# Two-layer backbone with experts: the norms' affine parts and the modulation as per-partition scale and offset on ScalarE, and the next layer's first chunks behind the experts

## Chip, cores, metric

One core of a Trainium2 chip. The metric is the device time of one execution in microseconds, the median of the runs. The core's engines work from queues of their own: TensorE (PE in the profile, its weight loads PEld), VectorE (DVE), ScalarE (ACT), GpSimd (POOL) and SyncE (SP), which here only issues DMA. They meet in semaphores. All data is float32.

## What is computed

256 latent tokens (`x`) and 256 context tokens (`ctx`), 1024 wide, go through two layers. `c` and `c_ctx` give the modulation vectors of the two streams. The reference, cut:

```python
for l in range(DEPTH):                     # DEPTH = 2
    mod_x = (c_act @ w_ada[l] + b_ada[l])[:, None, :]      # 6 vectors of 1024
    mod_c = cc_act @ w_ada[l] + b_ada[l]
    sh1, sc1, g1, sh2, sc2, g2 = jnp.split(mod_x, 6, axis=-1)
    px = _modulate(x, sh1, sc1) @ w_in[l]                  # h * (1 + scale) + shift
    ...   # Fourier mixer | differential attention | spatial gating -> mix_x
    x = _layernorm(DEEPNORM_ALPHA * x + g1 * (mix_x @ w_out[l]), ln_g[l, 0], ln_b[l, 0])
    ...   # the same for ctx, but in the last layer
    hx = _modulate(x, sh2, sc2)
    yx = _moe(hx, _route(hx, w_router, router_bias), moe_w1[l], moe_w3[l], moe_w2[l])
    x = _layernorm(DEEPNORM_ALPHA * x + g2 * yx, ln_g[l, 1], ln_b[l, 1])
return x
```

`_layernorm` subtracts the mean, divides by the root of the variance and applies `* g + b`, its affine part. `_moe` sends each token to 2 of 16 experts.

## The kernel before

**Tiling.** The tokens lie in `X` as four tiles of 128 rows (0 and 1 latent, 2 and 3 context); `tiles(L)` is 4 in layer 0 and 2 in layer 1, whose context output nobody needs, though its keys and values are needed. A tile is scaled and shifted into `H` (`HR`), turned on TensorE in eight 128x128 pieces into PSUM, copied into `XT` by ScalarE, and then multiplied with weights. PSUM's eight banks go round by a plan (`plan_layer`, `make_plan`): a job is named ("hT", L, t, half), ("ada", L, chunk) and so on; `full` waits for a job's result, `read` for its bank to be read out.

**Weights** come through a ring of six slots of 2 MB (`ring_plan`, `SLOTS`), loaded by SyncE in the ring's order; a load waits until the last job on its slot is done. A layer uses 12 chunks of `w_ada` (512 columns each: 0 and 1 are shift 1, 2 and 3 scale 1, 4 and 5 gate 1, 6 and 7 shift 2, 8 and 9 scale 2, 10 and 11 gate 2), the five chunks q, k, g, f, v of `w_in`, two of `w_out`, and then the 16 experts, whose three weights of 2 MB use three slots each, two experts at a time. The first four chunks of layer 1 stand, before, ahead of layer 0's experts in the ring and on TensorE.

**Modulation.** A chunk product (L1301, L1305) leaves a row of 512 values for the two streams; VectorE or ScalarE copies it to `R4`; `spread` (L1291) multiplies it by a selecting column, which repeats it over 128 partitions, one product of 128x512 for each stream; ScalarE copies that (L703) to `SH`, `SCL` or `GT`, which lie in `RA`, `RB` and `RC`. VectorE scales a tile (`modulate`, L929), GpSimd adds the shift (`shift`, L587).

**Norms.** For each tile VectorE sums up (`stats`, L938 to L934), GpSimd takes the root (L574), VectorE normalises (L946) and multiplies by `ln_g` (L949), GpSimd adds `ln_b` (L579); the vectors lie spread in `LNR` (`KT`). `norm_steps` writes the order out by hand, the same on VectorE and GpSimd: for the norm after the experts, tile n's mixing stands ahead of tile n-1's normalisation and tile n-2's modulation.

**Experts.** After `route` (L1468) and some 60 small operations on VectorE, GpSimd scatters each token's modulated row to two places of the DRAM table `xg_rows` (L605, one issue for each tile and choice), waits, reads blocks of 32 rows back (L615), ScalarE stages them, TensorE turns them (L1510), multiplies up (L1520) and down (L1536), and GpSimd stores the results in `y_rows` (L619). In the end it gathers each token's two rows into `G2` (L658), and VectorE mixes them (L1252 to L1256). Both tables are filled once at the start from `X` (L670, L672).

## Time and profile before

| | us |
|---|---|
| median of 3 runs | 1348.96 |
| lowest and highest | 1346.81, 1351.88 |
| the profiled execution, its own time | 1349.48 |
| its span, first to last instruction | 1347.9 |

| engine | busy us | share of the span |
|---|---|---|
| TensorE, products | 1009.5 | 75% |
| VectorE | 371.5 | 28% |
| GpSimd | 333.1 | 25% |
| ScalarE | 249.2 | 18% |

The DMA engines moved 332.08 MB, 246 GB/s in the mean. The profile is one execution; its time stands half a microsecond over the median. A share of busy time is a mean over stages that have different limits, so it has to be read by stage: from the timeline of an engine (each row is one or more equal instructions, with the idle time ahead of them and what ended it), and from windows, which give the busy time of each engine in a stretch.

### The profile page before, as it was taken

How to read it: one execution, taken by the hardware profiler on the slowest of the kernel's cores; microseconds unless marked ns; L12 is line 12 of the kernel's file. 1: busy time of each engine (PE TensorE's matmuls, PEld its weight loads, DVE VectorE, ACT ScalarE, POOL GpSimd, SP SyncE). 2: the span in 40 equal slices, each digit the busy share in tenths (PEclk: the TensorE clock that was granted, in tenths of full speed). 3: DMA queues.
4: the chain of work that ended last, by engine and by line, in shares of the span. 5: the costliest groups of instructions: out<-in, count | busy, mean ns of one | idle time of the engine just before them, and what ended most of it. 6: DMA issues, size and time to landing. Idle time of an engine off the chain costs nothing.

```text
span 1347.9 us, 23928 instructions
## 1 busy us (share of the span) xinstructions
PE 1009.5 (75%) x8962; PEld 550.3 (41%) x8963; DVE 371.5 (28%) x780; ACT 249.2 (18%) x519; POOL 333.1 (25%) x521
## 2 busy tenths in 40 slices
PE   3799998999839989977766408998893666865860
PEld 0444655445415545544434204455333333432430
DVE  0420228245302122211111186215243111101215
ACT  0211129301212112211110101115300111201110
POOL 1400000113333434332231345000022222321333
PEclk9899999999869999998798658999995888987995
DMA  9992310734764766689899770331684799999952
GB/s 301 392 414 71 125 63 1 269 137 146 284 257 146 261 257 224 211 304 331 327 388 408 284 244 29 124 125 63 246 317 186 283 399 401 357 395 406 394 191 94
DMA packets 91426, 332.08 MB, mean 246 GB/s; under 512 B 12988, under 2 KB 15164, under 8 KB 66804
## 3 DMA queue, kind: packets, MB, share of 16 engines
q1 hardware_dynamic: 68436, 282.05, 55.2%
q0 software_dynamic: 21472, 48.27, 10.5%
q10 hardware_dynamic: 1472, 1.12, 0.3%
q8 instruction: 32, 0.52, 0.2%
q14 instruction: 14, 0.11, 0.0%
HBM read 303.88 MB, written 27.53 MB: 246 GB/s over the span
## 4 chain that ended last, share of the span: by engine, by line
PE 60%; DMA 15%; issue 9%; DVE 8%; POOL 3%; SPq 3%; ACT 2%; POOLq 0%; DVEq 0%; ACTq 0%
PE PS L1520 18%; PE PS L1345 15%; DMA W<-in_moe_w 10%; PE PS L1536 7%; PE PS L1457 6%; PE PS L1510 3%; PE PS L1316 2%; PE PS L1301 2%; DMA xg_rows<-H,DEST 2%; PE PS L1528 1%; SPq L534 1%; PE PS L1291 1%; DMA X<-in_ctx 1%; ACT EX L785 1%; PE PS L1468 1%
## 5 line engine op out<-in xcount | busy, mean ns | idle before, releaser
L1520 PE MATMUL PS<-W,XT 128*32 128x256 f32 x4224 | 284.7, 429 | 114.9 <-DMA W<-in_moe_w 62.9
L1520 PEld LDWEIGHTS PS<-W,XT 128*32 128x32 f32 x4224 | 153.6, 123 | 224.5 <-issue 156.5
L619 POOL DMA_DIRECT2D y_rows<-H x264 | 130.9, 497 | 383.1 <-DVE H L1194 356.2
L1345 PE MATMUL PS<-W,XT 128*128 128x512 f32 (+1 forms) x544 | 218.3, 562 | 2.7 <-ACT RB L703 1.8
L1345 PEld LDWEIGHTS PS<-W,XT 128*128 128x128 f32 x544 | 104.1, 193 | 111.7 <-issue 109.4
L1536 PE MATMUL PS<-W,AT 128*32 128x256 f32 x2112 | 130.6, 389 | 3.6 <-DVE AT L1191 3.6
L1184 DVE COPY EX<-PS 128x256 f32<-128x256 f32 x66 | 28.0, 424 | 338.8 <-PE PS L1520 338.8
L703 ACT ACTIVATE H<-H 64x512 f32<-64x512 f32 x70 | 44.1, 631 | 361.3 <-PE PS L1510 318.5
L1510 PE MATMUL PS<-C,H 64*128 64x64 f32 x272 | 46.1, 291 | 66.7 <-ACT H L703 36.2
L615 POOL DMA_DIRECT2D H<-xg_rows x148 | 73.7, 501 | 74.0 <-issue 32.9
L1457 PE MATMUL PS<-W,XT 128*128 128x512 f32 x192 | 83.1, 593 | 0.0
L595 POOL TENSOR_TENSOR RSTD<-VAR,HALF 128x1 f32<-128x1 f32 (+1 forms) x12 | 9.6, 804 | 289.0 <-DVE VAR L934 289.0
L1536 PEld LDWEIGHTS PS<-W,AT 128*32 128x32 f32 x2112 | 63.3, 111 | 43.1 <-issue 5.7
L1510 PEld LDWEIGHTS PS<-C,H 64*128 64x128 f32 x272 | 37.6, 209 | 96.0 <-issue 96.0
L1301 PE MATMUL PS<-W,CT 128*32 128x512 f32 x384 | 53.1, 676 | 23.4 <-DMA W<-in_w_ada 23.4
L703 ACT ACTIVATE XT<-PS 128x512 f32<-128x512 f32 (+1 forms) x46 | 23.4, 541 | 203.7 <-PE PS L1316 189.8
L1194 DVE COPY H<-PS 128x256 f32<-128x256 f32 x66 | 28.0, 425 | 112.1 <-PE PS L1536 112.1
L1457 PEld LDWEIGHTS PS<-W,XT 128*128 128x128 f32 x192 | 36.3, 190 | 45.0 <-issue 45.0
L1187 DVE COPY XT<-PS 128x256 f32<-128x256 f32 x68 | 28.9, 424 | 88.3 <-PE PS L1510 88.3
L1316 PE MATMUL PS<-C,EX 128*128 128x128 f32 x88 | 16.0, 299 | 46.0 <-DMA EX<-in_sgu_w 33.7
L587 POOL TENSOR_TENSOR H<-H,RA 128x1024 f32<-128x1024 f32 x14 | 36.4, 2607 | 45.7 <-DVE H L929 45.7
L703 ACT ACT_TABLE_LOAD x18 | 23.1, 1283 | 122.1 <-PE PS L1510 122.1
(170 smaller groups left out, 920.7 us busy)
## 6 DMA issues: line engine op xcount, KB each, us to landing
W<-in_moe_w SPq DMA_DIRECT2D x96, 2048.0 KB, 14.3
W<-in_w_ada SPq DMA_DIRECT2D x24, 2048.0 KB, 13.5
W<-in_w_in SPq DMA_DIRECT2D x8, 2048.0 KB, 17.1
H<-xg_rows POOLq DMA_DIRECT2D x148, 64.0 KB, 5.7
y_rows<-H POOLq DMA_DIRECT2D x264, 32.0 KB, 5.2
W<-in_w_out SPq DMA_DIRECT2D x4, 2048.0 KB, 9.8
xg_rows<-X POOLq DMA_DIRECT2D x1, 6656.0 KB, 31.1
y_rows<-X POOLq DMA_DIRECT2D x1, 4608.0 KB, 46.8
```

Of the source, the lines that this page charges most:

```text
L587: pool.tensor_tensor(HR[:, t, :], HR[:, t, :], SH[:, t // 2, :], ALU.add).then_inc(S[h + "_ready"], 1)
L615: pool.dma_start(XRAW[b][ROWS * q:ROWS * q + ROWS, :], part_of_rows(xg_rows, n, slice(512 * q, 512 * q + 512))) .then_inc(rows_in[b][L], 16)
L619: pool.dma_start(part_of_rows(y_rows, n, slice(256 * q, 256 * q + 256)), YO[b][ROWS * q:ROWS * q + ROWS, :]) .then_inc(y_written[b][L], 16)
L703: nc.scalar.activation(dst, src, ACT.Copy).then_inc(done, 1)
L1187: dve.tensor_copy(XGT, ROWS_PS[:, 0:8 * ROWS].rearrange("p (k s) -> p k s", k=4)).then_inc(xgt_ready[L], 1)
L1301: mm = pe.matmul(ps[a:a + 32, :], CT[:, k, :], w[:, k, :], start=(k < 4), stop=False, tile_position=(0, a))
L1316: mm = pe.transpose(ps[:, P * n:P * n + P], piece, IDENT)
L1345: mm = pe.matmul(ps[:, 0:cw], XT[:, k, P * t:P * t + P], w[:, k, :], start=(k == 0), stop=(k == KD - 1))
L1457: mm = pe.matmul(ps, XT[:, k, P * t:P * t + P], w[:, k, :], start=(k == 0), stop=(k == KD - 1))
L1510: mm = pe.transpose(ROWS_PS[:, 2 * ROWS * k:2 * ROWS * k + 2 * ROWS], turned[:, k, :], IDENT[0:2 * ROWS, 0:2 * ROWS])
L1520: mm = pe.matmul(UP_PS[o:o + ROWS, 0:256], rows, moe_up(3 * p + n)[:, k, 256 * a:256 * a + 256], start=(k == 0), stop=(k == KD - 1), tile_ ...
L1536: mm = pe.matmul(DOWN_PS[o:o + ROWS, 0:256], rows, moe_down(3 * p + 2)[:, k, 256 * q:256 * q + 256], start=(k == 0), stop=(k == FE // P - ...
```

## The change

The scale and offset of a modulation become columns: one value for each of the 128 features that lie on the partitions once a tile is turned. So the raw tile of `X` is turned, and ScalarE applies both when it copies each 128x128 piece out of PSUM (`modulated`). For a tile that comes out of a norm, the norm's `ln_g` and `ln_b` are folded into them. The chunks 4, 5, 10 and 11, the gates, are still spread to rows; the other eight become columns by four products of two columns each (`spread`, `columns`).

`X` itself is only normalised (L976 of the changed kernel). Its affine part and the factor ALPHA are applied later, by two passes of VectorE on each tile (`residual`): after the router in both layers, and in layer 1 after the rotations. The rows for the scatter are got by turning `XT` back (jobs "hx") and copying them to `HR` on ScalarE. The last norm of all applies its affine part in two passes on VectorE. GpSimd has no passes over tiles left. ScalarE weighs the first of the two gathered rows (`weigh`). The first four chunks of layer 1 are loaded and multiplied behind the experts of layer 0. The group weights ("ab", "swT") stand ahead of the chunks in layer 0 and behind the first projections in layer 1. The norm vectors for the second norm are loaded within the experts (`load_ln`), and the fills of the tables no longer stand behind four shifts on GpSimd.

```diff
@@ ring_plan, plan_layer
     for L in range(DEPTH):
-        if L == 0:
-            for c in range(4):
-                put(("ada", L, c))
+        for c in range(4):
+            put(("ada", L, c))
...
         put(("ada", L, 10)), put(("ada", L, 11))
-        for c in range(4 if L + 1 < DEPTH else 0):
-            put(("ada", L + 1, c))
...
-    if L + 1 < DEPTH:
-        jobs += ada([0], L + 1)
+    jobs += [("hx", L, t, hf) for t in range(T) for hf in range(2)]
     jobs += [("rk", L), ("ct", L)]
-    if L + 1 < DEPTH:
-        jobs += ada([1, 2, 3], L + 1)
@@ SyncE
+            for n, vec in enumerate((ln_g, ln_b)):
+                o = 2 * DEPTH * KD * n
+                sp.dma_start(LNV[o:o + 2 * DEPTH * KD, :], vec.rearrange("l j (k p) -> (l j k) p", p=P)).then_inc(ln_cols_in, 16)
...
-                    sp.wait_ge(done, steps_of_layer(sp, L0))
+                    sp.wait_ge(done, steps_of_layer(sp, L0) if s >= 3 else steps_before(sp, L0, NEXP - 1))
@@ GpSimd
+            def load_ln(L, j):
+                if j:
+                    pool.wait_ge(S["affine"], val("affine", L, 0))
+                pool.dma_start(LNR[:, 0, :], ln_g[L, j].partition_broadcast(P)).then_inc(ln_in, 16)
+                pool.dma_start(LNR[:, 1, :], ln_b[L, j].partition_broadcast(P)).then_inc(ln_in, 16)
...
-                if L == 0:
-                    for t in range(4):
-                        shift("h1", 0, t)
...
+                load_ln(L, 1)
                 pool.wait_ge(meta_ready, L + 1)
...
                 for t in range(T):
                     if t >= 2:
+                        rstd(req(L, "ln2", t - 2), 1)
                         pool.wait_ge(S["mixed_ready"], val("mixed_ready", L, t - 2))
@@ ScalarE
+            def modulated(key, kind, t):
+
+                ps = full(act, key)
+                hf = key[3]
+                for k in range(4):
+                    n = 4 * hf + k
+                    ins = nc.scalar.activation(XT[:, n, P * t:P * t + P], ps[:, P * k:P * k + P], ACT.Identity,
+                                               bias=MB[:, kind, n, t // 2:t // 2 + 1], scale=MA[:, kind, n, t // 2:t // 2 + 1])
+                ins.then_inc(freed(key), 1)
...
+                g0 = G2[:, t % 2, 0, :]
+                nc.scalar.activation(g0, g0, ACT.Copy, scale=WK2[:, t, 0:1]).then_inc(weighed, 1)
...
+                if L:
+                    ada_rows(L, [0, 1, 2, 3])
+                    weigh(L - 1, 0)
+                    weigh(L - 1, 1)
...
+                gates(L, [10, 11])
+                for t in range(T):
+                    for hf in range(2):
+                        key = ("hx", L, t, hf)
+                        copy(HR[:, t, 512 * hf:512 * hf + 512], full(act, key), freed(key))
@@ VectorE
-                link(dve.tensor_scalar(X[:, t, :], X[:, t, :], MV[:, t, 0:1], RSTD[:, r, 0:1], ALU.subtract, ALU.mult))
...
+                dve.tensor_scalar(X[:, t, :], X[:, t, :], MV[:, t, 0:1], RSTD[:, r, 0:1], ALU.subtract, ALU.mult)\
+                    .then_inc(done, 1)
+
+            def residual(L, j, t):
+
                 dve.wait_ge(ln_in, 32 * (2 * L + j + 1))
-                dve.tensor_tensor(X[:, t, :], X[:, t, :], LNR[:, 0, :], ALU.mult).then_inc(done, 1)
+                link(dve.scalar_tensor_tensor(out=X[:, t, :], in0=X[:, t, :], scalar=ALPHA, in1=LNR[:, 0, :],
+                                              op0=ALU.mult, op1=ALU.mult))
+                return dve.scalar_tensor_tensor(out=X[:, t, :], in0=LNR[:, 1, :], scalar=ALPHA, in1=X[:, t, :],
+                                                op0=ALU.mult, op1=ALU.add)
...
+                for t in range(T):
+                    mix(t)
+                    if t == 0 and L + 1 < DEPTH:
+                        for c_ in range(4):
+                            columns(L + 1, c_)
+                    normalise(L, "ln2", t, S["ln2_norm"])
@@ TensorE
+                if not is_row(c_):
+                    ps, done = claim(("col", L, c_))
+                    for m in range(4):
+                        mm = pe.matmul(ps[:, 2 * m:2 * m + 2], R4[:, c_ % 2, P * m:P * m + P], cst("sel"), start=True, stop=True)
+                    mm.then_inc(done, 1)
+                    return
...
-                            turn(("hT", L, t, hf), [HR[:, t, 512 * hf + P * k:512 * hf + P * k + P] for k in range(4)])
+                            turn(("hT", L, t, hf), [X[:, t, 512 * hf + P * k:512 * hf + P * k + P] for k in range(4)])
```

**Three places in the order.** First SyncE's loads from layer 0's chunks 4 to 9 to the experts, before and after; W is the ring, in_w_ada the chunks, in_moe_w the experts' weights.

```order
L534 DMA W<-in_w_ada 128x8x512 x6
L534 DMA W<-in_w_out 128x8x512 x2
L534 DMA W<-in_w_ada 128x8x512 x6
L491 DMA W<-in_moe_w 128x2x2048 x6
L510 UNCONDITIONAL_BRANCH
```

```order
L538 DMA W<-in_w_ada 128x8x512 x6
L538 DMA W<-in_w_out 128x8x512 x2
L538 DMA W<-in_w_ada 128x8x512 x2
L492 DMA W<-in_moe_w 128x2x2048 x6
L514 UNCONDITIONAL_BRANCH
```

Four loads, layer 1's first chunks, are gone from ahead of the experts' first six; they stand now behind the loop's end.

Second, TensorE from the last tile's turning (PS<-C,H, then PS<-C,X) to the experts' first turned rows (PS<-C,H 128x64); GATE marks the rank and count products.

```order
L1316 MATMUL PS<-C,H 128x128 x8
L1468 MATMUL PS<-WR,XT 128x16 x16
L1301 MATMUL PS<-W,CT 32x512 x8
L1305 MATMUL PS<-BA,C 32x128 x4
L1291 MATMUL PS<-R,C 128x512 x2
L1493 MATMUL PS<-GATE,C 128x16
...
L1497 MATMUL PS<-GATE,C 128x16 x4
L1301 MATMUL PS<-W,CT 32x512 x8
L1305 MATMUL PS<-BA,C 32x128 x4
```

```order
L1363 MATMUL PS<-C,X 128x128 x8
L1526 MATMUL PS<-WR,XT 128x16 x16
L1363 MATMUL PS<-C,XT 128x128 x32
L1552 MATMUL PS<-GATE,C 128x16
...
L1556 MATMUL PS<-GATE,C 128x16 x4
L1567 MATMUL PS<-C,H 128x64 x4
```

The chunk products on either side of the ranks are gone, and 32 turnings of XT, the rows for the scatter, stand in the place of the first.

Third, VectorE at the handover, from the first gathered tile; G2 lies in H, WK holds the two weights of a token, MA, MB and SHC are the columns.

```order
L1252 TENSOR_SCALAR H<-H,WK 128x1024
L1253 SCALAR_TENSOR_TENSOR H<-H,WK 128x1024
L1255 TENSOR_TENSOR H<-H,RC 128x1024
L1256 SCALAR_TENSOR_TENSOR X<-X,H 128x1024
L938 BN_STATS ST<-X 128x6 x2
L940 BN_AGGR MV<-ST 128x2
L934 TENSOR_SCALAR VAR<-MV 128x1
...
L946 TENSOR_SCALAR X<-X,MV,RSTD 128x1024
L949 TENSOR_TENSOR X<-X,KT 128x1024
L1252 TENSOR_SCALAR H<-H,WK 128x1024
```

```order
L1297 SCALAR_TENSOR_TENSOR H<-H,WK 128x1024
L1299 TENSOR_TENSOR H<-H,RC 128x1024
L1300 TENSOR_TENSOR X<-X,H 128x1024
L961 BN_STATS ST<-X 128x6 x2
L963 BN_AGGR MV<-ST 128x2
L957 TENSOR_SCALAR VAR<-MV 128x1
L938 COPY SHC<-PS 128x8 x2
...
L953 TENSOR_TENSOR MB<-MB,SHC 128x8
L976 TENSOR_SCALAR X<-X,MV,RSTD 128x1024
L1297 SCALAR_TENSOR_TENSOR H<-H,WK 128x1024
```

Before, tile 1's seven rows stand where the dots are, ahead of tile 0's normalisation. After, only the eight small operations on the columns stand there, and tile 1 comes behind.

## Rows read from the trace of the kernel before

**Rows 1.** The page's part 4: the chain that ended last, shares by engine.
```profile
PE 60%; DMA 15%; issue 9%; DVE 8%; POOL 3%; SPq 3%; ACT 2%; POOLq 0%; DVEq 0%; ACTq 0%
```

**Rows 2.** Timeline of the start: start us, us, engine, line, operation, [idle before <-releaser].
```profile
42.69 8.92 DVE L929 SCALAR_TENSOR_TENSOR H<-RB,X 128x1024 f32<-128x1024 f32 x4 [3.64 <-DMA X<-in_ctx]
...
52.35 8.13 PE L1345 MATMUL PS<-W,XT 128*128 128x512 f32 x16
...
56.06 1.20 POOL L670 DMA_DIRECT2D xg_rows<-X  x1
```

**Rows 3.** The scatters: POOL's timeline, and in layer 0 the hardware queue of 355:400.
```profile
361.59 1.05 POOL L605 DMA_INDIRECT xg_rows<-H,DEST  x1 [20.43 <-issue]
...
389.57 0.60 POOL L615 DMA_DIRECT2D H<-xg_rows  x1 [18.11 <-DMA xg_rows<-H,DEST]
...
q1 hardware_dynamic: 851, 6.45, 35.9%
...
1043.65 2.07 POOL L615 DMA_DIRECT2D H<-xg_rows  x4 [3.35 <-DMA xg_rows<-H,DEST]
```

**Rows 4.** Timelines of the handover between the layers: PE and DVE.
```profile
735.30 3.66 PE L1520 MATMUL PS<-W,XT 128*32 128x256 f32 x64
...
777.92 0.75 DVE L1252 TENSOR_SCALAR H<-H,WK 128x1024 f32<-128x1024 f32 x1 [13.10 <-DMA H<-y_rows,DEST]
...
784.11 0.15 DVE L934 TENSOR_SCALAR VAR<-MV 128x1 f32<-128x1 f32 x1
...
792.70 0.81 DVE L946 TENSOR_SCALAR X<-X,MV,RSTD 128x1024 f32<-128x1024 f32 x1 [2.19 <-POOL RSTD L574]
...
795.48 3.25 DVE L1253 SCALAR_TENSOR_TENSOR H<-H,WK 128x1024 f32<-128x1024 f32 x1
...
811.11 1.97 PE L1316 MATMUL PS<-C,H 128*128 128x128 f32 x8 [13.73 <-POOL H L587]
813.96 9.67 PE L1345 MATMUL PS<-W,XT 128*128 128x512 f32 x16 [0.89 <-ACT XT L703]
...
843.75 41.48 PE L1345 MATMUL PS<-W,XT 128*128 128x512 f32 x112 [1.81 <-ACT RB L703]
```

**Rows 5.** Windows: stretch, length, busy of five engines, PEclk, DMA share, GB/s.
```profile
1080.00:1120.00 40.00, 20.17 (x282) 11.04 (x278) 4.70 (x12) 5.29 (x8) 10.20 (x21) 0.87 1.02 403
```

**Rows 6.** Loads of W issued by SyncE from 28 to 30: issue to landing.
```profile
DMA to landing us min/median/max: 19.7/21.7/23.6
```

**Rows 7.** Queues, packets, MB, share: from 60 to 61, then from 62 to 63.
```profile
q0 software_dynamic: 11, 0.05, 11.7%
...
q0 software_dynamic: 70, 0.29, 69.6%
q1 hardware_dynamic: 67, 0.14, 35.2%
```

**Rows 8.** PE's timeline in layer 0: chunk products, router, last tile, counts.
```profile
249.41 1.98 PE L1291 MATMUL PS<-R,C 128*128 128x512 f32 x4
...
312.37 1.86 PE L1468 MATMUL PS<-WR,XT 128*128 128x16 f32 x16
...
340.17 1.09 PE L1316 MATMUL PS<-C,H 128*128 128x128 f32 x8 [1.50 <-POOL H L587]
...
355.34 1.87 PE L1497 MATMUL PS<-GATE,C 128*128 128x16 f32 x8
```

**Rows 9.** ACT's timeline: one 128x128 piece out of PSUM with a scale.
```profile
943.25 0.37 ACT L803 ACTIVATE RB<-PS,RI 128x128 f32<-128x128 f32 x1
```

**Rows 10.** PE's timeline at the router of layer 1.
```profile
1013.63 1.94 PE L1316 MATMUL PS<-C,H 128*128 128x128 f32 x8 [4.91 <-POOL H L587]
1015.36 6.85 PE L1468 MATMUL PS<-WR,XT 128*128 128x16 f32 x32
```

**Rows 11.** The end: DVE's first pass and POOL's last.
```profile
1323.79 0.75 DVE L1252 TENSOR_SCALAR H<-H,WK 128x1024 f32<-128x1024 f32 x1 [13.13 <-DMA H<-y_rows,DEST]
...
1342.45 2.34 POOL L579 TENSOR_TENSOR X<-X,KT 128x1024 f32<-128x1024 f32 x1 [1.16 <-DVE X L949]
```

More of the change, by code:

```diff
@@ L65 @@
 COUNTS = {
-    "h1_ready": lambda L: 4,
     "q_rot": lambda L: 2, "k_rot": lambda L: 2,
@@ L415, in backbone, with g_wait @@
         passed = sem("passed")
+        def g_wait(eng, L, t):
+            eng.wait_ge(g_in[t % 2], 32 * (sum(tiles(l) for l in range(L)) // 2 + t // 2 + 1))
         def wait_apart(eng, semaphore, value):
@@ L979, in _ @@
                 dve.tensor_copy(SWT[:, :, :].rearrange("p a b -> p (a b)"), full(dve, key)).then_inc(freed(key), 1)
+            key = ("lnc", 0)
+            dve.tensor_copy(LNC[:, :, :, :, :].rearrange("p a l j k -> p (a l j k)"), full(dve, key)[:, 0:4 * DEPTH * KD])\
+                .then_inc(freed(key), 1)
+            group_weights(0)
+            ada_copy(0, 0)
+            for c_ in range(1, 4):
+                ada_copy(0, c_)
+                columns(0, c_ - 1)
+            columns(0, 3)
+            for L in range(DEPTH):
+                T = tiles(L)
                 if L == 0:
@@ L994, in _ @@
                     rotate(KR, t).then_inc(S["k_rot"], 1)
+                if L:
+                    for t in range(T):
+                        read(dve, ("hT", L, t, 1))
+                        residual(L - 1, 1, t)
+                    group_weights(L)
                 for t in range(4):
@@ L1181, in _ @@
                 dve.tensor_copy(META[0:1, L, 2, 0:2], T2[0:1, :]).then_inc(halves_ready, 1)
+                for t in range(T):
+                    for hf in range(2):
+                        read(dve, ("xT", L, t, hf))
+                    ins = residual(L, 0, t)
+                ins.then_inc(S["affine"], 1)
                 def copy_up():
@@ new lines, in _, with mix @@
+                for c_ in (10, 11):
+                    for r in mod_streams(L, c_):
+                        read(dve, ("mod", L, c_, r))
+                def mix(t):
+                    g_wait(dve, L, t)
+                    dve.wait_ge(weighed, sum(tiles(l) for l in range(L)) + t + 1)
+                    g0, g1 = G2[:, t % 2, 0, :], G2[:, t % 2, 1, :]
+                    link(dve.scalar_tensor_tensor(out=g0, in0=g1, scalar=WK2[:, t, 1:2], in1=g0,
+                                                  op0=ALU.mult, op1=ALU.add))
+                    link(dve.tensor_tensor(g0, g0, GT[:, t // 2, :], ALU.mult))
+                    dve.tensor_tensor(X[:, t, :], X[:, t, :], g0, ALU.add).then_inc(S["mixed_ready"], 1)
+                    dve.wait_ge(S["mixed_ready"], val("mixed_ready", L, t))
+                    stats(L, "ln2", t)
```

311 lines of the change are left out of this document (143 added, 168 removed).

## The prediction

> **What bounds the kernel now.** I read the chain of waits first [rows 1]: TensorE carries 60% of it, DMA 15%, time in which nothing is seen to hold an engine 9%, VectorE 8%. So the kernel is mostly bound by the products, and I looked for the stretches where TensorE stands still, in the timeline of each engine. Five lie near the edit. (a) The start: the first projection begins at 52.35, although the tokens are in SBUF at 42.69 [rows 2]. (b) The two router stages, where the last tile's rows come late. (c) The scatter of the rows to the experts: in layer 0 first issue 361.59, rows read back 389.57; in layer 1 read back at 1043.65 [rows 3]. (d) The handover between the layers: TensorE turns the first rows of layer 1 only at 811.11, after 13.73 us of its last wait for GpSimd [rows 4]. (e) The end. Within the experts of layer 1 the bound is another: the DMA engines are 1.02 busy with 403 GB/s from 1080 to 1120 [rows 5]. That stream is driven by the products (a slot is reloaded when its expert is done), so experts that start earlier also end earlier.
>
> **Start.** Four scalings on VectorE (8.92 us together) and four additions on GpSimd lay between the tokens and the first turned rows [rows 2]. Now X itself is turned, and the scale and shift ride on ScalarE's copies out of PSUM. With the tokens at 42.7 two tiles are turned and tile 0 copied by about 47. The next wait is the weights of the chunk q. Their load was issued at 28.39 and took the shortest landing of its pair, 19.7 us, so 48.1 [rows 6]. And two things push it later. The two small loads of the norm vectors stand ahead of the weights on SyncE's queue: 0 to 1 us, I take 0.8. The two fills of the row tables, issued at 56.06 before [rows 2], now follow the tokens directly, at about 43. Between 60 and 61 their queue moved its first 0.05 MB, so bytes come about 4.5 us after the issue; between 62 and 63 it moved 0.29 MB and the weights' queue 0.14, packet for packet, so the weights keep a third [rows 7]. From 47.5 on the fills thus meet the last 1 us of q's load, which then takes 3. That puts q at 50.6 and the gain at **1.7**. Ends: q at 46.5 would be 5.8, and fills that move at once would give q at 56, a loss of 4.
>
> **Chunk products of layer 0 (4 to 9).** Six chunks each carried a spreading to rows of 1.98 us in two streams. Chunks 4 and 5, the gate, keep it. Chunks 6 to 9 become four products with 2 columns each. The nearest row is the router's, 128x128 by 16 columns: 1.86 us for 8 products, each in two passes [rows 8], so 0.93 for 4, and 0.85 net of overlap. Four times 1.98-0.93, all on TensorE's path: **4.2**. In layer 1 there is one stream, half of the row, so about **0.6**.
>
> **Router of layer 0.** TensorE waited 1.50 for GpSimd before the last tile [rows 8]; that goes, but ScalarE's part grows: a 128x128 piece with a scale takes 0.37 [rows 9], eight are 2.96 in the place of two copies. I take +0.7 (0 to 1.5). Then the rank and count products run after a pause, in which the chunk products had kept the clock up. In the trace the counts, 8 passes, took 1.87 while the router's 16 took 1.86 [rows 8], so a pass doubles; the 20 rank passes would lose 1.6. Together **-0.9**. The eight turned-back halves (hx) and their copies run beside VectorE's routing chain and cost nothing while they are done before the destinations, which come after the counts of 355.34 [rows 8].
>
> **Scatter of layer 0.** From the first issue to the rows read back there are 28.0 us, 9.9 of issues and 18.11 of waiting; in layer 1 the wait was 3.35 [rows 3]. The difference is 6.45 MB of weights that ran on the hardware queue in that stretch [rows 3]: three of the first six expert slots were held by the chunks of layer 1, which stood there. Now these chunks come behind the experts, so the six slots are filled as chunks 8 to 11 and the two output chunks are used, all before the last tile is turned at 340.17 [rows 8]; even four loads of 2 MB from there, at 400 GB/s [rows 5], are over by 361. The scatter then has the engines alone: 9.9 of issues, 3.35, and 1.0 for bytes that fall behind the issues over twice the tiles, 14.3. The gain is **13.7** (7 to 15). What is late next is VectorE: it now multiplies X by the norm's vectors and ALPHA there, 2 passes a tile. Eight passes at about 1.3 (tile 0's 6.3 us of mixing and statistics in [rows 4] hold five such steps) are 10 us, done before the rows are read back. If each took 3.25, as one does beside GpSimd's own work [rows 4], they would last 26 and end 12 us late.
>
> **Handover.** Before, tile 0's rows were there at 777.92 and its statistics done at 784.26 [rows 4], 6.3 us later; then the normalisation waited until 792.70, since it stood behind tile 1 on VectorE and behind two gathers on GpSimd, and scaling, offset, modulation and shift of four tiles shared the two engines, one of VectorE's passes growing to 3.25 [rows 4]. After: gathered rows at 779.3 (1.4 later, since 14 MB of weights are now asked for instead of 6 and share the engines); the first weighting on ScalarE 1.1 (bounds 0.75, VectorE's time for it [rows 4], and 2.96); the rest of the mix and the statistics 5.5; eight small column operations 2; normalisation 0.81. Turned rows at 788.9 instead of 811.1. From turned rows to the first projection it took 2.85 and now 4.4 (the eight pieces), so 793.3 instead of 813.96: 20.7. From there to the 112 records at 843.75 it took 29.8, of which 27 were products (9.67, two of 7 and three turnings of 1.1); tiles now follow each other every 7.2 us on VectorE against 8 on TensorE, so about 2.9 of waits go, and the group products that had stood in the idle time, 1.7, come in. Sum **21.9** (12 to 27). Cover: the four chunk products must be done by then. Their loads no longer wait for the last expert: the first two leave when expert 14's up product is done, 739.0 [rows 4], the next after its down product, which I put 16 us later; two loads of 5.1 us at 400 GB/s [rows 5] bring the fourth chunk by about 769, some 10 before the gathered rows, and q by 781. SyncE's loads of the chunks f and v wait for the gathers as before.
>
> **Router of layer 1.** TensorE turned the last rows at 1013.63 after waiting 4.91 for GpSimd, and the router products took 6.85 for 32 records, twice the rate of [rows 8], at the lower clock after the pause [rows 10]. Now the rows are there before the chunk products end, so 4.9 go; without a pause the products take 3.7, another 3.1; ScalarE's pieces and the first half's overlap give net 0.1. **8.1** (4 to 9).
>
> **Norm vectors.** Their second load, 1 MB, ran in the idle DMA of the router stage; now it is issued behind the third store of the experts. In layer 0 there is room; in layer 1 the stream is full [rows 5], and 1 MB at 400 GB/s is **-2.6** (0 to -3.5).
>
> **End.** From gathered rows at 1323.79 to the end of GpSimd's last addition, 1342.45+2.34, there are 21.0 [rows 11]. After: 1.1 of ScalarE, then per tile 5.5, about 1.2 for the root, and two passes of 1.25, 18.4 for both tiles, 19.5 in all, **+1.3**.
>
> **The sum.** 1.7+4.2+0.6-0.9+13.7+21.9+8.1-2.6+1.3 = 48.0. The profiled execution took 1349.5, half a microsecond above the median of the runs, so I forecast 1301.5 and round to **1301**.
>
> **Rule against trace.** The scatter issues of [rows 3] ran with VectorE idle, about 1.05 each, and no row shows one beside a pass over X, as they now stand. The Trainium skill (SBUF — State Buffer, A bandwidth-pool intuition that's wrong, and the box on the DVE blocking DMA) says that a DMA issued from GpSimd needs descriptors which GpSimd can't write while VectorE holds the shared port in a 2-port mode. By that rule in its widest reading each issue waits for one pass, 1301 would become 1311 to 1316, and the first rival below goes by it; its page names copies and tensor-scalar forms, not these.
>
> **Rivals.** (1) VectorE's passes collide with GpSimd's scatter issues, either way round. Eight issues held back by 1.25 each are 10 us in layer 0 and 5 in layer 1, or the passes grow to 3.25 and end late by as much. For it: the 3.25 of [rows 4]. Against it: that one came beside GpSimd's arithmetic. Time 1311 to 1316. (2) Layer 1 waits for its chunk weights: gathers, stores and 14 MB share the engines, and TensorE's and ScalarE's queues stand behind the fourth chunk. If the weights keep a third of 400 [rows 7] from 755 on, 4 MB take 31 us, the fourth chunk lands near 786, and 10 to 13 us of the handover are lost: 1311 to 1314. (3) The handover is better than this: the rows come no later, and the start gains 5: 1288 to 1294. (4) **Slower than before**: the wait of (2) taken to its end. ScalarE must copy four chunks before it may weigh tile 0, and VectorE needs their columns before it normalises; every microsecond by which the fourth chunk lands after 776 (its product and copy take some 3) is one on the path. It decides from 48 us past that, a landing at 824; one at 860 gives 1385. Only a slot that is released late could do it; the 14 MB queued there are 35 us of bytes from 739, which speaks against it. (5) The change doesn't do what it says: the slots are released no earlier than before, or VectorE's passes eat the gain: 1343 to 1354.
>
> **How the numbers follow.** Forecast, 1293 to 1309: 0.61. Rival 1: 0.09; rival 2: 0.13; rival 3: 0.10; both 1 and 2 or half the handover, 1316 to 1342: 0.02; rival 4: 0.02; rival 5: 0.03, of which 0.02 within the bound. The range, 1290 to 1317, takes in the forecast, rivals 1 and 2 and part of 3, with the ends of the scatter, the start and the handover. What a measurement of this kernel can tell from no change is 0.5%, 6.7 us. Faster 0.95, same 0.02, slower 0.03.
>
> **What would show it.** In the changed kernel's timeline: the first projection near 50 and its release by DMA; rows read back 14 us after the first scatter issue in layer 0, with no weights on the hardware queue; layer 1's first turned rows at 11 to 12 us after the gathered rows; no pass of 3.25 on VectorE; router records of layer 1 at half the time; the distance of the last gather to the end 1 to 2 us shorter. Wrong would be: a 128x128 piece on ScalarE far above 0.37, TensorE waiting for in_w_ada in the handover, or VectorE not done when the first rows of the experts are turned.

## The result, and the profile after

The changed kernel takes **1298.61 us** (median of four runs, 1297.23 to 1299.59) against 1349.88 in the same rounds (1346.81 to 1351.88): a ratio of 0.9635, 95% interval 0.961 to 0.9661. A second timing (x_ref below) gave 1295.57 and 0.9604 (0.9586 to 0.9621). The forecast was 1301, range 1290 to 1317, and faster. The profiled execution took 1297.62 with a span of 1296.0, so 51.9 of span are gone where the sum had 48.0.

Put beside each other, the marks of the two traces give this (us; each is the distance between two marks before, less the same distance after):

| step | forecast | the two traces |
|---|---|---|
| start, up to the chunk products of layer 0 | 1.7 | 2.8 |
| chunk products, layer 0 | 4.2 | 4.2 |
| router, layer 0 | -0.9 | -0.5 |
| scatter, layer 0, to the first turned rows | 13.7 | 12.3 |
| experts, layer 0 | (0) | 7.9 |
| handover, from the first gather to the end of layer 1's attention | 21.9 | 22.3 |
| chunk products, layer 1 | 0.6 | 1.2 |
| output projection and router, layer 1 | 8.1 | 5.5 |
| scatter, layer 1 | (0) | -1.7 |
| experts, layer 1 | -2.6 | -4.4 |
| end | 1.3 | 2.3 |

The page's chain of the changed kernel, which answers to [rows 1]: VectorE has lost half of its share, GpSimd a third, and DMA has grown.

```profile
PE 63%; DMA 17%; issue 9%; DVE 4%; SPq 3%; ACT 2%; POOL 2%; POOLq 0%; DVEq 0%; ACTq 0%
```

The marks are, in order: TensorE's first chunk product of layer 0 behind the attention, its first output projection product, GpSimd's first scatter issue, the experts' first turned rows, the first gather's issue, and the same again in layer 1, up to the span's end.

The start, in the timelines of GpSimd (the first fill) and TensorE (the first projection); [rows 2] had them at 56.06 and 52.35.

```profile
42.76 1.18 POOL L664 DMA_DIRECT2D xg_rows<-X  x1 [35.18 <-DMA X<-in_ctx]
...
47.62 10.01 PE L1398 MATMUL PS<-W,XT 128*128 128x512 f32 x16 [2.67 <-DMA W<-in_w_in]
```

The projection is 4.7 sooner and released by its weights, as forecast, but at 47.6 and not at 50.6. It then ran slower (10.01 for 16 products against 8.13), which took a part back.

The scatter of layer 0, GpSimd's timeline and under it three of VectorE's eight residual passes; it answers to [rows 3].

```profile
355.11 1.75 POOL L597 DMA_INDIRECT xg_rows<-H,DEST  x1 [30.12 <-issue]
357.16 2.00 POOL L597 DMA_INDIRECT xg_rows<-H,DEST  x1 [0.30 <-issue]
359.46 0.95 POOL L597 DMA_INDIRECT xg_rows<-H,DEST  x1 [0.30 <-issue]
360.71 0.95 POOL L597 DMA_INDIRECT xg_rows<-H,DEST  x1 [0.30 <-issue]
361.97 1.97 POOL L597 DMA_INDIRECT xg_rows<-H,DEST  x1 [0.30 <-issue]
...
371.12 2.08 POOL L607 DMA_DIRECT2D H<-xg_rows  x4 [3.42 <-DMA xg_rows<-H,DEST]
```

```profile
354.68 1.23 DVE L982 SCALAR_TENSOR_TENSOR X<-X,KT 128x1024 f32<-128x1024 f32 x1
...
357.08 1.22 DVE L982 SCALAR_TENSOR_TENSOR X<-X,KT 128x1024 f32<-128x1024 f32 x1
...
361.90 1.21 DVE L982 SCALAR_TENSOR_TENSOR X<-X,KT 128x1024 f32<-128x1024 f32 x1
```

From 355 to 390 this queue moved all but 0.05 MB; the hardware queue, which had 6.45 MB in [rows 3], moved nothing:

```profile
q0 software_dynamic: 1808, 5.38, 44.7%
```

The wait for the scatter's bytes is 3.42 instead of 18.11, close to the 3.35 of layer 1 before. But three of the eight issues are 0.8 to 1.1 us longer than the 0.95 of their neighbours. VectorE's passes keep their 1.23 and are over at 364.4, 10.9 before VectorE is wanted.

The handover, in time: the third and the fourth chunk product (TensorE), its copy and the first weighting (ScalarE), the first turned rows and the first projection (TensorE). It answers to [rows 4].

```profile
743.04 3.54 PE L1348 MATMUL PS<-W,CT 128*32 128x512 f32 x16 [2.00 <-DMA W<-in_w_ada]
...
748.42 1.92 PE L1348 MATMUL PS<-W,CT 128*32 128x512 f32 x16 [0.50 <-DMA W<-in_w_ada]
```

```profile
750.76 0.60 ACT L688 ACTIVATE R<-PS 128x512 f32<-128x512 f32 x1 [3.16 <-PE PS L1352]
754.45 1.15 ACT L731 ACTIVATE H<-H,WK 128x1024 f32<-128x1024 f32 x1 [3.10 <-DMA H<-y_rows,DEST]
```

```profile
763.36 1.97 PE L1363 MATMUL PS<-C,X 128*128 128x128 f32 x8 [10.79 <-DVE X L976]
767.73 10.05 PE L1398 MATMUL PS<-W,XT 128*128 128x512 f32 x16 [2.40 <-ACT XT L718]
```

The first gather is issued at 744.50, so it is 18.9 us to turned rows, where it was 40.0 (771.16 to 811.11). The rows themselves come later after the issue, 9.95 instead of 6.76.

The experts, windows from the first turned rows to the first gather, both layers; columns as in [rows 5]. First the kernel before, then the changed one.

```profile
393.30:771.16 377.86, 299.01 (x4194) 173.70 (x4194) 66.03 (x172) 67.56 (x107) 127.68 (x258) 0.90 0.76 281
1047.27:1317.03 269.76, 183.18 (x2554) 102.58 (x2554) 39.55 (x101) 41.28 (x65) 76.34 (x155) 0.89 0.91 352
```

```profile
374.52:744.50 369.98, 297.09 (x4250) 166.32 (x4254) 65.97 (x172) 68.64 (x109) 128.86 (x260) 0.92 0.79 293
993.34:1267.48 274.14, 187.35 (x2554) 103.46 (x2554) 39.52 (x101) 42.56 (x66) 77.48 (x156) 0.87 0.90 351
```

The largest surprise is the first column after the stretch: 7.9 less in layer 0 and 4.4 more in layer 1, though the edit puts nothing into these loops but one load of norm vectors. The granted clock goes the same way, 0.90 to 0.92 and 0.89 to 0.87. Whether that is the kernel or the execution is what the first experiment asks.

### The profile page after: what moved, and what is told of

Its sections match the earlier page's. It is cut to its first block, busy times and chain, and to the rows that moved or that the text cites. A ratio compares the mean times of both kernels' runs of the same rounds, so it can differ in the third digit from the quotient of the medians.

```text
span 1296.0 us, 24219 instructions
## 1 busy us (share of the span) xinstructions
PE 1008.2 (78%) x9083; PEld 558.1 (43%) x9084; DVE 336.0 (26%) x795; ACT 271.3 (21%) x594; POOL 268.1 (21%) x495
## 4 chain that ended last, share of the span: by engine, by line
PE 63%; DMA 17%; issue 9%; DVE 4%; SPq 3%; ACT 2%; POOL 2%; POOLq 0%; DVEq 0%; ACTq 0%
PE PS L1577 17%; PE PS L1398 17%; DMA W<-in_moe_w 13%; PE PS L1593 7%; PE PS L1515 7%; PE PS L1567 3%; PE PS L1348 2%; PE PS L1363 2%; DMA W<-in_w_in 1%; PE PS L1585 1%; SPq L538 1%; POOL xg_rows L597 1%; DMA H<-y_rows,DEST 1%; ACT EX L785 1%; PE PS L1526 1%
## 5 line engine op out<-in xcount | busy, mean ns | idle before, releaser
L1577 PE MATMUL PS<-W,XT 128*32 128x256 f32 x4224 | 280.3, 424 | 116.3 <-DMA W<-in_moe_w 64.6
L1577 PEld LDWEIGHTS PS<-W,XT 128*32 128x32 f32 x4224 | 145.5, 122 | 229.8 <-issue 162.1
L580 POOL TENSOR_TENSOR RSTD<-VAR,HALF 128x1 f32<-128x1 f32 (+1 forms) x24 | 16.3, 683 | 480.1 <-DVE VAR L957 480.1
L718 ACT ACTIVATE XT<-PS,MB,MA 128x128 f32<-128x128 f32 x112 | 40.5, 470 | 142.4 <-PE PS L1363 142.4
L851 ACT ACTIVATE EX<-PS 128x128 f32<-128x128 f32 x66 | 18.3, 277 | 76.1 <-PE PS L1585 75.9
L1585 PE MATMUL PS<-C,EX 128*128 128x128 f32 x132 | 33.6, 337 | 0.0
```

Of the source, the lines that this page charges most:

```text
L718: ins = nc.scalar.activation(XT[:, n, P * t:P * t + P], ps[:, P * k:P * k + P], ACT.Identity, bias=MB[:, kind, n, t // 2:t // 2 + 1], scal ...
L1577: mm = pe.matmul(UP_PS[o:o + ROWS, 0:256], rows, moe_up(3 * p + n)[:, k, 256 * a:256 * a + 256], start=(k == 0), stop=(k == KD - 1), tile_ ...
L1585: mm = pe.transpose(TURN_PS[:, P * k:P * k + P], turned[:, k, :], IDENT)
```

## Experiments

All are edits of the changed kernel but for the second execution of the kernel before. Spans of a stretch are distances between the marks of the table.

**The same kernel twice more.** No edit.

> The changed kernel once more, without an edit, for a second profiled execution. Between the kernels before and after the products of the experts took TensorE 297.2 us before and 289.3 after in layer 0, and 183.2 before and 187.4 after in layer 1, with the same number of products. Theory A: which products fall into the lower clock follows from the kernel's own order and waits, so this execution shows 289.3 and 187.4 again, within 0.5. Rival B: it changes from execution to execution by single products of 1.7 to 2.5 us, and the two numbers differ from those by one or several of such steps.

> The kernel before once more, without an edit, for a second profiled execution. In four profiled executions in which the experts of layer 0 are word for word the changed kernel's, the time from their first turned rows to the first gather was 370.0, 372.2, 373.5 and 377.5 us; the one trace of before shows 377.9. Theory: this spread, of single products at the lower clock, covers the kernel before too, and this execution shows 370 to 378. Rival: before is slower there for a reason of its own, and it shows 377 to 379. In layer 1 (269.8 before, 272.5 to 274.1 after) the same question: 269 to 271 if the second norm vectors' load is what makes the difference, up to 274 if it is chance.

> The changed kernel without an edit, timed in the same rounds as the three kernels beside it, so that they can be compared with it and not only with the kernel before. Expected: 1296 to 1300, and in the profiled execution again three scatter issues of 1.7 to 2.0 us in layer 0 and two in layer 1, 16.0 and 9.9 from the first issue to the rows read back, 272 to 275 for the experts of layer 1, and for the experts of layer 0 anything from 370 to 378, since that varied so over eight profiled executions of the same instructions.

The same two windows of x_same:

```profile
373.39:745.56 372.17, 302.83 (x4262) 168.51 (x4266) 66.03 (x172) 68.75 (x109) 128.71 (x259) 0.91 0.79 293
992.79:1265.33 272.54, 187.59 (x2554) 103.53 (x2554) 39.57 (x101) 42.55 (x66) 77.47 (x156) 0.87 0.91 353
```

Theory A of x_same fell: layer 0 took 372.17 with TensorE busy 5.7 longer than in the first execution. Over the eleven profiled executions with the changed kernel's expert loops in layer 0, the stretch took 370.0 to 377.7, mean 374.5. The kernel before took 377.9 and, in x_before, 377.8. Chance is a large part of that spread: x_qgate and x_noln below run the changed kernel's instructions word for word up to the end of this stretch, and took 372.8 and 377.5. So the 7.9 of the table can't be read as a gain of the edit; the first trace is the shortest of the eleven. Nor is it shown to be chance alone. The three executions of the unedited changed kernel are the three shortest of the eleven (370.0, 370.7, 372.2), the two of before agree within 0.1, and the distance of the two means, 374.5 and 377.8, is some 3. How much of the 7.9 belongs to the kernel stays open.

The same holds for the output projection of layer 1. Its first 27 to 29 us, in the first trace and in x_same:

```profile
923.74:953.00 29.26, 29.26 (x67) 12.79 (x67) 7.11 (x14) 0.00 (x0) 0.56 (x1) 0.94 0.77 302
```

```profile
925.52:953.10 27.58, 27.58 (x67) 12.22 (x67) 7.11 (x14) 0.00 (x0) 0.56 (x1) 1.00 0.82 318
```

The same 64 products, TensorE without a pause in both, and a granted clock of 0.94 against 1.00: a part of that stretch ran at the lower of the two levels in one execution and not in the other. From the projection's start to VectorE's first routing operation it took 43.2 twice and 40.7 to 40.8 in nine executions, against 48.64 and 48.67 before. The term is then 7.9, where the forecast had 8.1 and the first trace seemed to say 5.5.

In layer 1's experts the difference is not chance, as the next experiment shows. x_ref again gave what was expected of it: 16.0 and 9.9 in the scatters, 370.7 and 272.9 in the experts.

**The norm vectors' second load left out in layer 1.**

```diff
-                load_ln(L, 1)
+                if L == 0:
+                    load_ln(L, 1)
...
-                    dve.wait_ge(ln_in, 32 * (2 * L + 2))
+                    dve.wait_ge(ln_in, 32 * (2 * L + 1))
```

> The changed kernel without the load of the second pair of norm vectors (1 MB) in layer 1; the last norm of the output is then done with the first pair's values, so that part is computed with other numbers. The prediction had priced this load at 2.6 us, as bytes in a full stream. Theory from the two traces: TensorE's idle time within the experts of layer 1 was 79.6 us before and 79.8 after, so the load costs nothing, and 1298 to 1299 comes out, with that idle time unchanged within 1 us. Rival, as predicted: 1 MB at 400 GB/s is on the path, the idle time falls by 2.6, and the time is 1296.

```profile
995.39:1265.94 270.55, 184.66 (x2554) 102.86 (x2554) 39.56 (x101) 42.55 (x66) 76.32 (x155) 0.88 0.90 351
```

1292.36 us, ratio 0.9582 (0.9567 to 0.9597). The experts of layer 1 took 270.55. With the load in the stream eight executions of them took 272.5 to 274.9 (mean 273.5); without it (this one, the two of before, x_clean and x_best, whose load stands ahead of the scatter) 269.8 to 271.8 (mean 270.9). The two sets don't overlap. The load costs about 2.6 us. The theory I had formed from the two traces, that it costs nothing since TensorE's idle time had not moved, was wrong; the term of the prediction, 2.6, was right. By the windows' first two columns, TensorE's idle time there was 87.2 in the mean of the eight and 85.6 in the mean of the five, its busy time 186.3 and 185.3: 1.6 of the price is idle time and 1.0 busy time. But single executions of the eight lay anywhere from 85.0 to 88.6 of idle time, so two traces could not show it. In time, 1292.36 is 3 to 6 us below the two timings of the changed kernel.

**The chunks ahead of the experts again.** The ring, the plan and the four products go back to their old places, the columns stay.

```diff
-        for c in range(4):
+        for c in range(4 if L == 0 else 0):
             put(("ada", L, c))
...
         put(("ada", L, 10)), put(("ada", L, 11))
+        for c in range(4 if L + 1 < DEPTH else 0):
+            put(("ada", L + 1, c))
```

> The changed kernel with its second part undone: the four chunk products of layer 1, their loads and their column operations stand ahead of the experts of layer 0 again, one before the ranks and three after the counts; the columns and the affine parts stay as they are. Theory: the shorter scatter of layer 0 comes from this move alone, since three expert slots are no longer held by the chunks. So from the first issue to the rows read back it takes 26 to 30 us instead of 16.0, and the experts' first rows are turned 10 to 14 later. At the handover the gathered rows come 1 to 3 sooner, since fewer weights are asked for with them. Together 1305 to 1312. Rival: the scatter became shorter because the norm vectors' loads left that stretch; then it stays at 16 and the time is 1296 to 1300.

GpSimd's timeline, and the hardware queue from 355 to 390:

```profile
363.97 1.95 POOL L603 DMA_INDIRECT xg_rows<-H,DEST  x1 [0.30 <-issue]
...
384.14 2.09 POOL L613 DMA_DIRECT2D H<-xg_rows  x4 [16.96 <-DMA xg_rows<-H,DEST]
```

```profile
q1 hardware_dynamic: 816, 6.29, 45.0%
```

1307.57 us, ratio 0.9692 (0.9677 to 0.9707). From the first issue to the rows read back it takes 27.9 instead of 16.0, with 6.29 MB of weights on the hardware queue, as in [rows 3]. From the routing's start to the first turned rows it is 50.5 against 36.6. Of these 13.9, 11.9 are the scatter and the other 2.0 lie before it, where a chunk product again stands ahead of the ranks. The gathered rows of the handover come 6.6 after their issue again. So the move brings the whole gain of the scatter and costs 3.3 at the handover. Only one issue is long here, since VectorE's first pass began only at 363.86.

**VectorE's passes away from the scatter,** in two steps. x_early takes all tiles' passes out of the scatter but the last one's:

```diff
                     normalise(L, "ln1", t, S["ln1_norm"])
+                    if t:
+                        for hf in range(2):
+                            read(dve, ("xT", L, t - 1, hf))
+                        residual(L, 0, t - 1)
...
-                for t in range(T):
-                    for hf in range(2):
-                        read(dve, ("xT", L, t, hf))
-                    ins = residual(L, 0, t)
-                ins.then_inc(S["affine"], 1)
+                for hf in range(2):
+                    read(dve, ("xT", L, T - 1, hf))
+                residual(L, 0, T - 1).then_inc(S["affine"], 1)
```

> The changed kernel with VectorE's two passes over X (norm vectors and ALPHA) taken out of the scatter: for all tiles but the last they stand behind the next tile's normalisation, beside the output projection, and only the last tile's two passes stay where they were. Theory: some of GpSimd's scatter issues took 1.75 to 2.0 us instead of 0.95 because VectorE ran these passes beside them. Three of eight in layer 0 and two of four in layer 1 would go back to 0.95, apart from one or two beside the last tile's passes: 1 to 2 us less in layer 0 and 0 to 1.7 in layer 1, so 1295 to 1297. Rival: the issues are long for another reason (the first ones after a long idle, or ScalarE's copies into the rows); they stay at 1.75 to 2.0 and the time is 1298 to 1299.

x_clean moves the last tile's too, ahead of the routing chain, and `load_ln(L, 1)` from the third store to a place before the scatter:

```diff
-                load_ln(L, 1)
...
                 rstds(L, "ln1")
+                load_ln(L, 1)
...
+                    for n in (t - 1, t) if t == T - 1 else (t - 1,) * (t > 0):
+                        for hf in range(2):
+                            read(dve, ("xT", L, n, hf))
+                        ins = residual(L, 0, n)
+                ins.then_inc(S["affine"], 1)
...
-                for t in range(T):
-                    for hf in range(2):
-                        read(dve, ("xT", L, t, hf))
-                    ins = residual(L, 0, t)
-                ins.then_inc(S["affine"], 1)
```

> The changed kernel with all of VectorE's residual passes ahead of the routing chain, the last tile's too (VectorE stands idle for 9 us there while the last tile is turned and its router product runs), and the load of the second norm vectors issued before the scatter, as in the kernel before, since those passes are over by then. Theory: no issue of the scatter is beside a pass any more (28.0 became 16.0 and now 14.3 in layer 0; 9.9 becomes 8.2 in layer 1), and the experts of layer 1, 272.5 to 274.1 with the load in them, take 270 to 271. Together 5 to 7 less than the changed kernel: 1291 to 1294. Rival: the passes ahead of the routing delay it by up to 2.5 in each layer, and the load of 1 MB, now ahead of the scatter, costs nothing there; then 1296 to 1298.

GpSimd's timeline in x_clean, the first issue and the read:

```profile
352.98 1.05 POOL L597 DMA_INDIRECT xg_rows<-H,DEST  x1 [14.51 <-issue]
...
366.96 2.10 POOL L607 DMA_DIRECT2D H<-xg_rows  x4 [4.09 <-DMA xg_rows<-H,DEST]
```

In x_early only the first issue of each layer stayed long (1.74 and 1.98), beside the last tile's passes; the scatters took 14.65 and 9.17. In x_clean none was longer than 1.05, and they took 13.98 and 8.24 instead of 16.0 and 9.92. The passes lay in VectorE's idle time: from the output projection's start in layer 0 to the first scatter issue it took 91.4 in x_clean and 92.8 in x_best, which has the same passes, and 91.6 to 93.6 in the executions with the passes left or moved less (x_ahead aside). In layer 1 the same stretch took 53.7 in both, against 53.6. The experts of layer 1 took 271.8. x_early was timed at 1297.24 (0.9614, 0.9593 to 0.9634), which the runs can't tell from the changed kernel; x_clean at 1293.47 (0.9587, 0.9563 to 0.9611), inside its theory, but its interval overlaps those of the changed kernel (0.961 to 0.9661 and 0.9586 to 0.9621). That it gains rests on the stretches of the trace.

**The fills later.**

```diff
                     pool.wait_ge(x_in, 32)
+                    pool.wait_ge(w_full[PLACE["in", 0, "q"][0]], 16 * PLACE["in", 0, "q"][1])
```

> The changed kernel with the two fills of the row tables issued only when the weights of the first projection have landed. Theory, as predicted: at the end of that load the fills share its queue's engines and stretch its last microsecond to three; without them the first projection starts 1.5 to 2.5 earlier, near 45, released by ScalarE's pieces at the soonest, and the time is 1.5 to 2.5 below the changed kernel's, 1294 to 1297. Rival: the load is late for its own queue (the ten loads ahead of it), and the start stays at 46.7 to 48.9, as in five profiled executions of the changed start.

TensorE's and GpSimd's timelines:

```profile
47.12 10.15 PE L1399 MATMUL PS<-W,XT 128*128 128x512 f32 x16 [2.21 <-DMA W<-in_w_in]
...
47.71 1.18 POOL L665 DMA_DIRECT2D xg_rows<-X  x1 [40.13 <-DMA W<-in_w_in]
```

1300.61 us, ratio 0.9634 (0.9609 to 0.966): nothing gained. The fills now start after the projection's weights are there, and the weights are there at the same time, 47.1, within the 46.7 to 48.9 of the other executions. So the fills are not what makes the load late. The rival's own cause, what stands ahead of the load on its queue, is what is left, but no run varied it.

**A later release of slots.**

```diff
-                    sp.wait_ge(done, steps_of_layer(sp, L0) if s >= 3 else steps_before(sp, L0, NEXP - 1))
+                    sp.wait_ge(done, steps_of_layer(sp, L0))
```

> The changed kernel with every expert slot released to layer 1's weights only after the last expert's step, as in the kernel before; the three slots of expert 14 thus wait one expert longer. Theory: the first chunk's load then leaves some 17 to 20 us later, the four chunks of 2 MB follow each other every 5.1, and the fourth, which landed at 748.4 with the rows weighed at 754.5, lands near 760. ScalarE copies the chunks ahead of its weighting, so the first weighting moves 7 to 11 back and the time is 1305 to 1310. Rival: the chunks' loads are not what the handover waits for (three of them go out at once when the step is over), and it is 1299 to 1302.

TensorE (the fourth chunk product) and ScalarE (the weightings):

```profile
765.12 3.64 PE L1348 MATMUL PS<-W,CT 128*32 128x512 f32 x16 [7.11 <-DMA W<-in_w_ada]
```

```profile
769.90 2.18 ACT L731 ACTIVATE H<-H,WK 128x1024 f32<-128x1024 f32 x2
```

1307.66 us, ratio 0.9685 (0.9663 to 0.9707). From the gather's issue to the weighting it took 17.7 instead of 9.2 to 10.5, and the weighting starts with the end of the fourth chunk's copy, not with a wait for the gathered rows. That copy ended 6.9 behind the gather's issue in the first trace and 17.8 here, 10.9 later; 3.1 were margin and the other 7.8 are on the path. This is the mechanism of the rival "slower than before" at a small dose, in this one dose one for one beyond the margin. The release of three slots one expert earlier, a single expression in the diff, is worth 8 us of the handover in the trace (167.9 up to layer 1's chunk products, against 159.6 to 160.1 in the three executions of the changed kernel) and 12 in the times of the same rounds (1295.57).

**The weights of q held back,** and both good edits together (x_best: x_clean and this one).

```diff
+                if key == ("in", key[1], "q") and key[1]:
+                    sp.wait_ge(g_in[0], 32 * (sum(tiles(l) for l in range(key[1] - 1)) // 2 + 1))
                 if key == ("in", key[1], "f") and key[1]:
```

> The changed kernel with one more wait on SyncE's queue: in layer 1 the weights of the chunk q, and so all behind them, are issued only when tile 0's two gathered rows have landed. Theory: from the first gather's issue to the weighting it took 9.6 to 10.0 us, against 6.8 in the kernel before and 6.6 with the chunks ahead of the experts, because the weights asked for early share the engines; with q held back it takes 7.5 to 8.5. q is then asked for near 753 and lands by 762, before the first projection of 767.7 can start, so 1.5 to 2.5 are gained: 1295 to 1297. Rival: q becomes late itself, the first projection waits for its weights instead of ScalarE, and the time is 1299 to 1305.

> The two edits that did what was expected, together: all residual passes ahead of the routing with the second norm vectors' load before the scatter, and the weights of q in layer 1 held until tile 0's rows have been gathered. Theory: they act in different places and add, 4 to 6 for the first and 1.5 to 3 for the second, so 1289 to 1293, with 14.0 and 8.2 in the scatters, 7.2 from the gather to the weighting and 270 to 272 in the experts of layer 1. Rival: the fourth chunk's copy, which stood directly ahead of the weighting in the execution with q held back, takes the gain of the second edit, and the time is that of the first alone, 1292 to 1295.

ScalarE's timeline, x_qgate and then x_best:

```profile
755.92 0.60 ACT L690 ACTIVATE R<-PS 128x512 f32<-128x512 f32 x1 [2.62 <-PE PS L1354]
756.41 1.14 ACT L733 ACTIVATE H<-H,WK 128x1024 f32<-128x1024 f32 x1
```

```profile
753.79 1.15 ACT L733 ACTIVATE H<-H,WK 128x1024 f32<-128x1024 f32 x1 [1.79 <-DMA H<-y_rows,DEST]
```

x_qgate: 1295.95 us (0.9606, 0.9582 to 0.963), with 7.2 from the gather's issue to the weighting. There the fourth chunk's copy was already what the weighting waited for. Its time can't be told from the changed kernel's; the gain is one of the trace. x_best: **1289.26 us** (six runs, 1285.56 to 1297.01; ratio 0.9557, 0.9529 to 0.9586), beside 1295.57 for the changed kernel in the same rounds; 14.0 and 8.2 in the scatters, 6.5 at the gather, 271.5 in the experts of layer 1. Against x_ref's trace its own stretches are 2.0+1.7+4.1+1.4 = 9.2 shorter, while the experts of layer 0 took 377.2 in that execution and 370.7 in x_ref's, the variation of above. It is clearly faster than the kernel before. Against the changed one it is 6.3 us in the medians, but the ends of the two intervals meet and single runs overlap.

## Why the prediction was right, and where it was not

**Start.** The direction and the releaser were right, the size not: 47.6 was measured where I had 50.6. The step that failed is "the weights keep a third": without the fills the load lands no sooner (x_fills), so they cost it nothing that shows. It was a loss computed from a rate 13 to 15 us later in the trace, [rows 7]; and by its own terms (48.1 and 0.8, bytes of the fills from 47.5) there were 1.4 us of load left to stretch and not 1, which gives 51.7. Over the executions the mark behind the start lies at 240.6 on the mean against 243.6 before, so 3.0.

**Chunk products and router of layer 0.** The 4.2 came out by luck in part: the four chunks' columns gave 3.6, and 0.6 came from the first chunk product of the stretch, which took 2.55 before and 1.92 after. The columns of a chunk took 1.05 for 8 passes where I had taken 0.93. The same holds for the 1.2 of layer 1, of which 1.0 is its first product (2.92 and 1.92), and it comes and goes between executions: the whole stretch took 19.3 in x_before and 20.4 in x_same. The router's -0.5 for -0.9 holds two errors that balance. 1.6 was gained up to the last turned tile (I had 1.5), then 1.4 was lost up to the ranks, where I had 0.7 for ScalarE's part, and the ranks lost 0.65, where I had 1.6. My own three terms add to -0.8.

**Scatter of layer 0.** The mechanism was right and is shown by x_ahead. The size was 12.3 instead of 13.7, 12.0 of it up to the rows read back: the wait after the issues was 3.4 and not 4.35, but the issues took 12.6 and not 9.9. That is the first rival, which I gave a chance of 0.09 at 10 to 15 us. It did happen, at 2.0 in layer 0 and 1.7 in layer 1 (x_clean), beside the forecast and not instead of it. I had treated it as a case that is there or not; it should have been a term with a size. Layer 1's part was nowhere in the sum. The rival's size failed as well: it had every issue wait for a whole pass, and three of eight waited for what was left of one.

**Handover.** 22.3 for 21.9. The pieces: weighting 1.15 (1.1), mixing and statistics 5.6 (5.5), columns 1.2 (2), turned rows to projection 4.4 (4.4). The rows came 3.2 later after their issue, where I had 1.4, and the columns gave 0.8 of that back, so 19.6 were gained up to the first projection for 20.7. The rest of layer 1's attention gave 2.7, where I had 1.2 (2.9 of waits less 1.7). The cover was thinner than I wrote: I had the fourth chunk some 10 before the gathered rows, and it was there 6 before, 3 with its product and copy. x_late shows what lay behind that margin. "TensorE waiting for in_w_ada in the handover" stood among the signs of being wrong, and it did wait, 2.00 and 0.50 us; it cost nothing, since the rows came 3.1 after the last copy. And the 11 to 12 us from gathered to turned rows, among the signs, doesn't follow from the sum, which has 9.6; 8.9 was measured.

**Router of layer 1.** 5.5 in the first trace, 7.9 in nine of eleven executions, for 8.1. **Norm vectors.** 2.6 forecast, about 2.6 measured over the executions; the 4.4 of the first pair holds 1.8 of chance. **Experts of layer 0.** No term of mine; 7.9 in the pair, and how much of it belongs to the kernel is open. **End.** 2.3 for 1.3: from the gathered rows to the last operation it took 18.9 where I had 19.5, since the second tile's weighting lay beside VectorE's work, and the last gathers came no later. The term was mis-subtracted too; 21.0 less 19.5 is 1.5.

So the sum, 48.0, came near to the 51.9 of the traces with errors that balanced by chance: the scatters gave 3.1 less than worked out, the first trace had the slow phase in the output projection against it (2.4), and it had 7.9 in its favour in a stretch in which one load was the only change. Over the three executions of the changed kernel the span is 51.9 to 54.2 below that of the first trace of before.

## What to carry to other kernels

When work for the next stage holds buffers that the present stage needs, moving it behind that stage can pay: here the slots were filled before the scatter, so that the scatter ran with no weights beside it (11.9 us). Look at once for what then shares the engines at the new place (3.3 us here), and for what must be released so that it arrives in time (12 us in x_late). Work that an engine takes over should lie where that engine is idle and where its neighbour issues no DMAs. And before a difference of a few us between two traces is explained, the same kernel is profiled again: here one stretch of some 374 us took from 370.0 to 377.5 in five executions that ran the same instructions up to its end.

## What the runs showed of the hardware

GpSimd's issue of an indirect DMA took 0.95 to 1.08 us beside no long VectorE pass. Beside the passes of `residual`, which read two streams of SBUF, it took 1.74 to 2.01 when it began 0.07 to 0.44 after the start of a pass (in the trace above 355.11 after 354.68, 357.16 after 357.08, 361.97 after 361.90; 363.97 after 363.86 in x_ahead; in layer 1 979.82 and 982.10, 0.20 and 0.07 after a pass). The excess is what was left of that pass: 0.8 left gave 1.75, 1.03 left gave 1.98, 1.15 left gave 2.01. Each of the 40 long issues in the nine traces that have them ended 0.82 to 0.96 after the end of the pass, the length of an undisturbed issue or a little less. So these issues looked blocked until the pass was over, and not slowed. An issue that began 0.01 ahead of a pass (359.46), or with less than 0.15 of one left, kept its 0.95 to 0.99, and the passes kept their 1.23.

The Trainium skill (SBUF — State Buffer, A bandwidth-pool intuition that's wrong, and the box on the DVE blocking DMA) says that GpSimd can't write descriptors while VectorE holds the shared port in a 2-port mode, which is the rule that the prediction named. The same page of the Trainium skill (Who interferes with whom) also has VectorE instructions with two SBUF inputs, which these passes are: they contend with a GpSimd instruction that reads SBUF, and the later of the two is blocked until the other is done. The trace has that pattern, and the prediction's "not these" overlooked it. Whether the issue of an indirect DMA, which takes its row numbers from `DEST`, counts as such a reading instruction the page doesn't say, and no run here separates it.

TensorE's granted clock fell to its lower level in other places from one execution of the changed kernel to the next, even within 64 products without a pause (0.94 against 1.00 above, 1.7 us). What sets the place was not found.
